# Rotated keys and queries of a second attention turned by VectorE blocks and GpSimd transfers instead of by TensorE

## The reference, cut to what matters

```python
k_shared = apply_rope_2((kv_in @ w_k).reshape(b, s, 16, 128), cos, sin)
v_shared = (kv_in @ w_v).reshape(b, s, 16, 128)
proj = hdn @ w_in_b[i]                # three groups of queries, then a gate
for g, (window, dilation) in enumerate(((128, 1), (512, 4), (2048, 16))):
    q = apply_rope_2(q_all[:, :, g], cos, sin)
    o_g, lse_g = dilated_window_attention(q, k_shared, v_shared, window, dilation)
```

## Time and profile before

| | |
|---|---|
| median of 3 runs | 2381.12 us (2380.31 to 2381.19) |
| profiled execution, its own time | 2380.03 us |
| its span, first to last instruction | 2378.3 us |
| mean granted TensorE clock | 0.999 |
| TensorE busy | 2360.8 us, 99% of the span |
| VectorE busy | 1627.4 us, 68% |
| ScalarE busy | 1121.9 us, 47% |
| GpSimd busy | 96.0 us, 4% |

### The profile page before, as it was taken

How to read it: one execution, slowest core, us unless ns; L and a number is a source line. 1 busy time by engine, 2 the same in 40 slices (tenths; PEclk the granted TensorE clock), 3 DMA queues, 4 the chain that set the end, 5 groups by cost and what they waited for, 6 DMA issues and landing times.

```text
span 2378.3 us, 30914 instructions
## 1 busy us (share of the span) xinstructions
PE 2360.8 (99%) x10907; PEld 1956.8 (82%) x10907; DVE 1627.4 (68%) x2016; ACT 1121.9 (47%) x1415; POOL 96.0 (4%) x194
## 2 busy tenths in 40 slices
PE   8999999999999999999999999999999999999998
PEld 6888788888888888888888888888888888888887
DVE  7998899899776656655544466666655557777664
ACT  4544545544464444444444454455544444444554
POOL 0001000000002112112100000000000000000000
PEclk9999999999999999999999999999999999999999
DMA  9985479999857877766655555565555554444454
GB/s 392 389 315 203 155 257 353 333 337 362 321 175 242 265 252 245 263 210 221 216 196 192 193 181 202 206 209 183 191 195 193 182 190 159 150 165 155 159 187 158
DMA packets 154132, 544.45 MB, mean 229 GB/s; under 512 B 19712, under 2 KB 21024, under 8 KB 153376
## 3 DMA queue, kind: packets, MB, share of 16 engines
q1 hardware_dynamic: 145584, 528.28, 63.4%
q10 hardware_dynamic: 2800, 8.81, 1.1%
q0 software_dynamic: 5632, 5.78, 0.8%
HBM read 534.91 MB, written 2.11 MB: 226 GB/s over the span
## 4 chain that ended last, share of the span: by engine, by line
PE 98%; DVE 1%; DMA 1%; ACT 0%; issue 0%; SPq 0%; ACTq 0%; DVEq 0%
PE acc L2050 30%; PE acc L2052 29%; PE acc L2051 29%; PE tb L2132 2%; PE tb L2573 1%; DMA start_raw<-in_wa_dram 1%; PE tb L2050 1%; PE tb L2051 0%; PE tb L2052 0%; PE acc L2100 0%; PE acc L2102 0%; PE acc L2101 0%; PE tb L2576 0%; PE tb L2319 0%; PE acc L2111 0%; DVE macc L1377 0%
## 5 line engine op out<-in xcount | busy, mean ns | idle before, releaser
L1186 DVE TENSOR_TENSOR lo<-raw,hi 128x1024 fp32r<-128x1024 f32 x809 | 969.3, 1207 | 596.1 <-ACT hi L590 593.6
L590 ACT ACTIVATE hi<-raw 128x1024 fp32r<-128x1024 f32 x809 | 843.3, 1049 | 943.9 <-PE acc L2052 759.5
L2050 PE MATMUL acc<-hi,Hh 128*128 128x512 f32 x1960 | 774.5, 395 | 1.2 <-DVE Hl L1729 0.7
L2052 PE MATMUL acc<-hi,Hl 128*128 128x512 f32 x1960 | 764.2, 390 | 0.0
L2051 PE MATMUL acc<-lo,Hh 128*128 128x512 f32 x1960 | 763.2, 389 | 0.0
L2050 PEld LDWEIGHTS acc<-hi,Hh 128*128 128x128 f32 x1960 | 368.1, 188 | 79.3 <-issue 4.4
L2052 PEld LDWEIGHTS acc<-hi,Hl 128*128 128x128 f32 x1960 | 367.9, 188 | 77.8
L2051 PEld LDWEIGHTS acc<-lo,Hh 128*128 128x128 f32 x1960 | 368.3, 188 | 75.5 <-issue 1.4
L2050 PE MATMUL acc<-hi,hbh 128*128 128x512 f32 x512 | 204.7, 400 | 0.0
L2052 PE MATMUL acc<-hi,hbl 128*128 128x512 f32 x512 | 200.2, 391 | 0.0
L2051 PE MATMUL acc<-lo,hbh 128*128 128x512 f32 x512 | 199.7, 390 | 0.0
(11 more groups left out here) (340 smaller groups left out, 2016.7 us busy)
## 6 DMA issues: line engine op xcount, KB each, us to landing
raw<-in_wa_dram SPq DMA_DIRECT2D x680, 512.0 KB, 4.4
late_raw<-in_wa_dram SPq DMA_DIRECT2D x96, 512.0 KB, 5.4
raw<-in_wb_dram SPq DMA_DIRECT2D x96, 512.0 KB, 4.1
start_raw<-in_wa_dram SPq DMA_DIRECT2D x64, 512.0 KB, 7.8
raw<-in_wc_dram SPq DMA_DIRECT2D x64, 512.0 KB, 3.4
tok<-sgt POOLq DMA_DIRECT2D x176, 32.0 KB, 5.0
x<-in_x_dram SPq DMA_DIRECT2D x2, 1024.0 KB, 6.0
gm<-gate_rows ACTq DMA_DIRECT2D x2, 1024.0 KB, 8.7
```

The source lines that it names most:

```text
L590: act.activation(hi[:, s, 0:n], raw[:, r, 0:n], ACT.Copy).then_inc(hi_ready, 1)
L1186: dve.tensor_tensor(lo[:, s, 0:n], raw[:, r, 0:n], hi[:, s, 0:n].bitcast(F32), ALU.subtract)\
L2050: pe.matmul(dst(tt), a, hi[:, s, w], start=first and i == 0, stop=False)
L2052: mm = pe.matmul(dst(tt), b, hi[:, s, w], start=False, stop=last and i == kts - 1)
```

## The change

DVE no longer hands rotated tiles to TensorE. It transposes their 32x32 squares from `tok` into `sgt`, in an order in which the four heads of a token lie beside each other (`head_minor`: token, half, head), and GpSimd moves the 16 blocks with transfers, as for the hidden tiles. `k2T` and the two `qT2` become tensors of token blocks. In them the tokens of one head stand 8 elements (32 bytes) apart, and TensorE reads both score operands in that step (`by_token`). TensorE's transposes of these tiles and ACT's copies of them are gone. Scores, and with them all that follows for a head, come four units later; DVE's and ACT's steps are put in a new order to match, and the gate tiles are turned at other units. DVE waits for the transfers of a tile before it writes `sgt` again.

```diff
-QUERIES_AT = {n: QB + 24 * (n // 3) + (13, 19, 27)[n % 3] for n in range(Q_TILES)}
-SCORES_AT = {h: QB + 24 * (h // Q_HEADS + 1) + 5 + 6 * (h % Q_HEADS) for h in range(HEADS2)}
+SCORES_AT = {h: QB + 24 * (h // Q_HEADS + 1) + 9 + 6 * (h % Q_HEADS) for h in range(HEADS2)}
-GATE_TURNED_AT = [GATE_B + 13, GATE_B + 19, GATE_B + 27]
+GATE_TURNED_AT = [GATE_B + 12, GATE_B + 18, GATE_B + 30]
+MOVED = 16 * 16
...
-        k2T = sb("k2T", [P, HEADS2, T], at=free)
+        k2T = sb("k2T", [P, HEADS2 // Q_HEADS, 4, TT * P], at=free)
...
+            for n in range(HEADS2 // Q_HEADS):
+                pool.wait_ge(key_blocks, n + 1)
+                for i in range(4):
+                    for j in range(4):
+                        pool.dma_start(k2T[32 * j:32 * j + 32, n, i, :], blocks_out[32 * i:32 * i + 32, j, :])\
+                            .then_inc(keys_moved, 16)
+            for n in range(Q_TILES):
+                b, g = divmod(n, NG)
+                if b > 1 and g == 0:
+                    pool.wait_ge(s_ready, HEADS1 + Q_HEADS * (b - 1))
+                pool.wait_ge(query_blocks, n + 1)
...
+                        pool.dma_start(qT2[b % 2][g][32 * j:32 * j + 32, i, :], blocks_out[32 * i:32 * i + 32, j, :])\
+                            .then_inc(queries_moved, 16)
...
-            with c.loop(act, 4, unit=16, raw=16, copy=2) as i:
-                split(6)
-                copy_tile(k2T, i * 4)
-                split(8)
+            with c.loop(act, 4, unit=16, raw=16) as i:
+                split(14)
...
+            def turn_blocks(out_of, done):
+                for tt in range(TT):
+                    ins = dve.transpose(out_of(tt), tok[:, 0, tt, :].rearrange("p (k j c) -> p j k c", k=4, j=4))
+                ins.then_inc(done, 1)
+            def head_minor(tt):
+                return blocks_out.rearrange("p j (t s k) -> p j s k t", s=TT, k=4)[:, :, tt]
...
-                rotate(0, lambda tt: tok[:, 0, tt, :], 4, HD, HD // 2, ropeC, ropeS)
-                split(11)
+                rotate(0, lambda tt: tok[:, 0, tt, :], 4, HD, HD // 2, ropeC, ropeS, done=keys_rotated)
+                split(1)
+                dve.wait_ge(keys_rotated, n + 1)
+                turn_blocks(head_minor, key_blocks)
+                split(10)
+                dve.wait_ge(keys_moved, n * MOVED + MOVED)
...
-                dve.wait_ge(tr_copy, copies_with(n - 1) if n else COPIES_BEFORE_K2 + 8)
-                rotate(n % 2, lambda tt: tok[:, 0, tt, :], 4, HD, HD // 2, ropeC, ropeS)
+                if n > 0:
+                    dve.wait_ge(queries_moved, MOVED * n)
+                rotate(n % 2, lambda tt: tok[:, 0, tt, :], 4, HD, HD // 2, ropeC, ropeS, done=queries_rotated)
+                split(1)
+                dve.wait_ge(queries_rotated, n + 1)
+                turn_blocks(head_minor, query_blocks)
...
-            tile(Hh, Hl, 1, 8, after={1: lambda: turned(0)})
+            tile(Hh, Hl, 1, 8)
...
+                if head == 0:
+                    pe.wait_ge(keys_moved, MOVED * (HEADS2 // Q_HEADS))
+                if head % Q_HEADS == 0:
+                    pe.wait_ge(queries_moved, MOVED * NG * (b + 1))
+                by_token = lambda ap: ap.rearrange("p i (t s k) -> p s k (i t)", s=TT, k=Q_HEADS)[:, :, at]
+                queries, keys = [by_token(qT2[b % 2][g]) for g in range(NG)], by_token(k2T[:, b])
...
-                    pe.matmul(tb[:, g // 2, (g % 2) * T:(g % 2 + 1) * T], q(g, P, P), k(T), start=True, stop=True)
+                    pe.matmul(tb[:, g // 2, (g % 2) * T:(g % 2 + 1) * T].rearrange("p (s t) -> p s t", s=TT), queries[g][:, 1], keys,
+                              start=True, stop=True)
...
-                for n in range(Q_TILES):
-                    if unit == QUERIES_AT[n]:
-                        turned_queries(n)
```

More of the change, by code:

```diff
@@ L333, in two_blocks @@
         mask2 = sb("mask2", [P, NG, T])
-        qT2 = [sb(f"qT2_{i}", [P, Q_HEADS * NG, T], at=h_at + i * 20 * KB) for i in range(2)]
+        qT2 = [[sb(f"qT2_{i}_{g}", [P, 4, TT * P], at=h_at + at * KB) for g, at in enumerate(ats)]
+               for i, ats in enumerate(((0, 4, 16), (8, 24, 28)))]
         att2 = sb("att2", [P, NG * 384])
@@ L370, in two_blocks @@
         tr_copy = sem("tr_copy")
+        keys_rotated = sem("keys_rotated")
+        key_blocks = sem("key_blocks")
+        keys_moved = sem("keys_moved")
+        queries_rotated = sem("queries_rotated")
+        query_blocks = sem("query_blocks")
+        queries_moved = sem("queries_moved")
         hid_blocks = sem("hid_blocks")
@@ L1059, in _ @@
                 split(2)
[L1061 to L1069, removed]
             def exponents(head):
@@ L1088, in gate @@
                 read_out(lambda tt: sgt[:, tt, :], i % 2, ACT.Silu, scaled=True)
-            for b in range(HEADS2 // Q_HEADS + 1):
+            for b in range(1, HEADS2 // Q_HEADS + 1):
                 head = Q_HEADS * (b - 1)
                 if b > 1:
+                    take_keys(head - 2)
+                    exponents(head - 1)
                     take_keys(head - 1)
-                if b > 0:
-                    take_queries(3 * b - 1)
-                    exponents(head)
                 if b == 4:
+                    act.wait_ge(queries_moved, MOVED * Q_TILES)
                     gate(0)
[L1099 to L1104, removed]
+                exponents(head)
+                take_keys(head)
+                if b == 4:
                     split_to(GATE_TURNED_AT[0] + 4)
                     take_hi_tile(Hh, 0)
-                if b > 0:
-                    take_keys(head + 1)
+                    gate(1)
+                exponents(head + 1)
+                take_keys(head + 1)
                 if b == 4:
[L1110 to L1115, removed]
                     split_to(GATE_TURNED_AT[1] + 4)
                     take_hi_tile(Hh, 4)
[L1118 to L1123, removed]
+                exponents(head + 2)
+            take_keys(HEADS2 - 2)
+            gate(2)
+            exponents(HEADS2 - 1)
             take_keys(HEADS2 - 1)
@@ L1283, in layer_norm_stats, with rotate @@
                 inverse_root()
-            def rotate(pair, dst, heads, dim, half, cos, sin, width=N, src=None):
+            def rotate(pair, dst, heads, dim, half, cos, sin, width=N, src=None, done=tok_ready):
                 h4 = lambda ap: ap.rearrange("p (h d) -> p h d", h=heads)
@@ L1768, in hidden @@
                     dve.wait_ge(acc_free[2 + tt], n + (TILES_BEFORE_OUT // 2 + 3))
[L1769 to L1772, removed]
+                turn_blocks(head_major, hid_blocks)
                 split(10)
@@ L1899, in _ @@
             chain(ins)
-            c.n["copy"] = COPIES_BEFORE_K2
-            with c.loop(dve, 4, unit=16, raw=16, copy=2, chain=2):
+            with c.loop(dve, 4, unit=16, raw=16, chain=2) as n:
                 split(5)
                 tile_done(3)
-                dve.wait_ge(tr_copy, c.at("copy"))
-                c.up("copy", 2)
-                rotate(0, lambda tt: tok[:, 0, tt, :], 4, HD, HD // 2, ropeC, ropeS)
-                split(11)
+                rotate(0, lambda tt: tok[:, 0, tt, :], 4, HD, HD // 2, ropeC, ropeS, done=keys_rotated)
[4 more added lines that the diff above has]
+                dve.wait_ge(keys_moved, n * MOVED + MOVED)
             dve.wait_ge(mask_loaded, 16)
@@ L1948, in attended @@
                                             None, ALU.mult)
-                ins.then_inc(tb_free[2], 1)
+                if head < HEADS2 - 1:
+                    ins.then_inc(tb_free[2], 1)
+                else:
+                    chain(ins)
+                    dve.sem_inc(tb_free[2], 1)
             def gated(i):
@@ L1961, in gated_lo @@
                 take_lo_tile(Hl, Hh, 4 * i)
-            for b in range(HEADS2 // Q_HEADS + 1):
+            turn_queries(0)
+            turn_queries(1)
+            for b in range(1, HEADS2 // Q_HEADS + 1):
                 head = Q_HEADS * (b - 1)
-                if b > 0:
-                    turn_queries(3 * b - 1)
+                turn_queries(3 * b - 1)
                 if b > 1:
+                    attended(head - 2)
+                    softmax(head - 1)
                     attended(head - 1)
-                if b > 0:
-                    softmax(head)
                 if b < 4:
@@ L1973, in _ @@
                 else:
+                    dve.wait_ge(query_blocks, Q_TILES)
                     gated(0)
-                if b > 0:
-                    attended(head)
+                softmax(head)
+                attended(head)
+                if b < 4:
                     softmax(head + 1)
-                if b == 4:
+                    turn_queries(3 * b + 1)
+                    attended(head + 1)
+                else:
                     gated_lo(0)
-                if b > 0:
+                    gated(1)
+                    softmax(head + 1)
                     attended(head + 1)
```

(21 more changed lines are left out.)

7 lines of the change are left out of this document (3 added, 4 removed).

## The result

The changed kernel takes 2401.84 us (median of 4 runs, 2401.10 to 2402.16); the kernel before, beside it on the same chip, 2380.72 us (4 runs). The ratio is 1.0089, with a 95% interval of 1.0077 to 1.0101: 21.1 us slower. The forecast was 2366.9 us, faster; the range reached to 2401, so the result lies outside it too, by 0.8 us.

What follows compares the result with a forecast made beforehand. TensorE's instruction list was taken to bound the kernel: 2380.03 us less 14.2 for the turns, all other terms 0, gave 2365.8, or 2366.9 as a median 1.1 higher (before: 2381.12). Range 2364 to 2401 us.

Steps and rivals of the forecast that it cites:

- What bounds the kernel: Whole kernel: as long as TensorE's list of instructions, TensorE being busy 99% of the span.
- The turns taken away: TensorE's transposes of 4 key and 12 query tiles: 0.89 us each, 14.2 us saved, all expected back.
- How TensorE reads: Score operands read at 32-byte steps: between 0 and 30.1 us more, taken as 0.
- Rival A: Score matmuls of 16 heads: strided reading halves TensorE's pace, 30.1 us more, 2397.0 us; chance 0.31.
- VectorE's transposes: Two added DVE transposes of 128x512 per tile: 0.69 us each taken, 1.2 as upper bound, beside TensorE's work.
- Waits and margins: DVE's splits and GpSimd's transfers in the query stage: expected in time for TensorE, cost taken as 0.
- the second split: Behind a block's second rotation and two transposes: ready 15.7, needed 16.6, margin 0.9 us; 0.2 late with transposes of 1.2.
- a tile transposed at 14.5: Second tile of a block: its transfers were to be in place at 27.6 to 29.4 us.
- VectorE's wait for transfers: Before rotating a block's third tile, DVE may wait 0.9 us; the split after it keeps a margin of 1.5.
- at the gate tiles: Gate product before the softmax may delay the probabilities: between 0 and 1 us, once, taken as 0.
- Rival B: Three blocks and gate tiles: DVE's long stretch makes splits late, giving back 2 to 8 us, about 2371; chance 0.07.
- the four units: Delaying scores leaves the third tile's transfers 7 to 9 us margin; four units less (10.9) would have used it up.

Runs made afterwards that it cites:

- b_moving_steps: The kernel before, with keys of the scores read at steps of 2, 4, 8 and 16 elements, one step per four heads: 2405.38 us, one run.
- b_moving_runs: The kernel before, with keys read in runs of two, four or 32 adjacent elements, or two from an odd element, per four heads: 2381.67 us, one run.
- v_contiguous: The changed kernel with keys in runs and queries contiguous, each GpSimd transfer scattering eight runs of 32 elements: 2368.40 us against 2380.43 before.

## Why the prediction was wrong

**What bounds the kernel** was right: in all eleven kernels the time follows TensorE's list to about 1 us, but for the waits of 0.3 and 1.8 us.

**The turns taken away, 14.2 us:** right; 13.8 with the reads undone.

**How TensorE reads: this step failed.** The prediction said "f32 asks for one only every 0.83, if it holds an element for its two passes", and took 0. It costs 35.7 us by the starts (35.2 came back with the reads undone). The 0.83 ns of an f32 column were rightly read from the earlier trace rows, but they don't show how often an element is fetched: a slow column can be one fetch with two passes or two fetches. I made the first reading the likeliest, with nothing in the rows that preferred it. The runs show 1.68 to 1.79 ns for an f32 column at steps 4 to 16, where fp32r has 0.84 to 0.90. The Trainium skill (SBUF — State Buffer, Door 1) had said it, two hits in a 16-byte line for full bandwidth, and b_moving_steps and b_moving_runs agree for f32; its remark that one may step 4 fp32 elements for free does not hold here: step 4 costs as much as step 8 (0.448 and 0.456 us). For fp32r even two hits are not enough. Why f32 costs twice fp32r's price from step 4 on, and not at step 2, stays open.

**Rival A** was the mechanism, with chance 0.31, and it sat at 2397.0. Its price, half pace, was called an upper bound and was too low: a record went up by factors of 2.13 and 2.09, not 2, and the change back to unit matmuls grew as well (0.44 us from the first to the second unit matmul, 0.31 before). 2.23 us a head for 1.88 is 5.6 us in all, and it put the result 0.8 us past the range's end.

**VectorE's transposes:** 1.16 us for 0.69 taken, inside my bounds, and within the estimate of 0.9 to 1.3 us from the Trainium skill (Vector Engine (DVE) Microarchitecture Reference, section 5.2). A step of 2 elements brought them to 0.687. It moved the end by nothing: with the reads undone all transposes are still long.

**Waits and margins:** right in sum, with two slips in the working. With transposes of 1.2 us the second split is ready at 13.15 + 2.40 + 1.13 = 16.7, so 0.1 late and not 0.2; and a tile transposed at 14.5 is in place at 27.3 to 29.1 by the earlier trace rows, not 27.6 to 29.4. With the reads undone no split came late: two long transposes hold VectorE up for 2.01 us, not 2.4 (2014.97 to the next split at 2016.98). VectorE's wait for transfers, allowed for with 0.9, was 0.5 us once in the changed kernel and 1.15 at most with the reads undone. No TensorE wait in the changed kernel; with the reads undone 0.3 us at the gate tiles, where 0 to 1 had been allowed. Rival B's mechanism showed once, in v_contiguous, and its cause was GpSimd's pause. That the four units are needed was not tried.

## What to carry to other kernels

Before an operand of a busy TensorE gets a new layout, price its access pattern, not its columns: keep at least two f32 elements in each 16 bytes for f32 matmuls and an fp32r moving operand contiguous, and look at the stationary operand apart, since at step 8 its load nearly hides under 256 columns (0.235 us for 0.215) and not under 128 (0.206 for 0.098). When the step is forced by the order in which tiles are written, write one operand in runs, as the keys here, which returned 23 of the 35 us; for the other let the transfers that move it anyway scatter, four pieces of 256 bytes a partition in place of one of 1 KB. That cost 52 ns an issue and returned the other 12 us. And where a row can be read in two ways, give the sign-deciding step no better than even odds and put the range's end beyond the simple bound.

## What the runs showed of the hardware that was not expected

- An f32 matmul's moving operand costs 0.84 to 0.89 ns a column contiguous, at step 2, or in runs of two and more, and 1.68 to 1.79 ns at steps 4, 8 and 16 (records of 256 columns). Step 16 was the cheapest of the three (0.429 us for 256 columns).
- The records of an fp32r matmul double (0.226 to about 0.45 us for 512 columns) in all six other patterns tried, pairs within 16 bytes among them.
- An f32 stationary operand at step 4 or 8 makes a record of 128 columns start 0.20 to 0.21 us after the last, 0.10 at steps 1 and 2.
- GpSimd's issue of a transfer depends little on its pieces: 497 ns for 32 pieces of 1 KB, 549 ns for 128 of 256 bytes, 583 ns for 256 of 128 bytes. Pauses within a tile's 16 transfers stand in the two scattering versions alone: one of 3.22 us in the first, three of 2.27, 6.06 and 4.38 us in the second. That the smaller pieces cause them is not shown.
- A STREAM_TRANSPOSE of 128x512 takes 0.687 us written at a step of 2 elements, as in contiguous runs (0.690), and 1.156 us at a step of 8.
